# Mixture-of-experts output added onto the residual in DRAM by accumulating scatters, second-normalisation statistics one tile ahead, and a sample output projection in four column tiles

## What is computed

```python
x = LayerNorm(alpha*x + concat(A, B) @ w_o)                 # first normalisation
x = LayerNorm(alpha*x + HMoE(x))                            # second normalisation
# HMoE: top-1 of 4 expert groups, then top-2 of the 8 experts in that group
def expert_mlp(args):
    xb, e = args
    h = jax.nn.silu(xb @ w_gate[e]) * (xb @ w_up[e])
    return h @ w_down[e]
```

## Time and profile before

| | us |
|---|---|
| median of 3 runs (2557.14 to 2563.7) | 2558.19 |
| the profiled execution, its own time | 2568.49 |
| its span, first to last instruction | 2566.7 |
| TensorE busy in the span | 2293.2 (89%) |
| VectorE, ScalarE, GpSimd busy | 648.8, 334.0, 276.3 |
| bytes moved | 534.87 MB, mean 208 GB/s |

### The profile page before, as it was taken

One profiled execution on the slowest core, in us unless ns is written; L12 is line 12 of the kernel. 1 busy time (PEld: TensorE's weight loads), 2 busy tenths in 40 slices (PEclk: granted clock), 3 DMA queues, 4 the chain that ended last, 5 costly groups with the idle time before them and its releaser, 6 DMA issues.

```text
span 2566.7 us, 30101 instructions
## 1 busy us (share of the span) xinstructions
PE 2293.2 (89%) x10192; PEld 1523.8 (59%) x10192; DVE 648.8 (25%) x1249; ACT 334.0 (13%) x827; POOL 276.3 (11%) x440
## 2 busy tenths in 40 slices
PE   7999899997999999998289998999889999999962
PEld 5666556665666666665156664566566666666641
DVE  1211234453111111111811123343521111111127
ACT  2000122210011111110110001222101111111101
POOL 0100001111111111110211000111001111111101
PEclk8999888997999999999589998898889999999985
DMA  7201010025899999995541101101259999999952
GB/s 251 103 33 33 17 45 33 33 103 233 319 382 378 381 373 379 371 376 214 208 150 33 33 33 29 41 33 66 114 222 354 375 384 373 374 377 379 376 215 107
DMA packets 104080, 534.87 MB, mean 208 GB/s; under 512 B 16570, under 2 KB 25786, under 8 KB 87266
## 3 DMA queue, kind: packets, MB, share of 16 engines
q1 hardware_dynamic: 89154, 500.04, 50.7%
q0 software_dynamic: 14848, 33.84, 3.6%
HBM read 506.86 MB, written 49.82 MB: 217 GB/s over the span
## 4 chain that ended last, share of the span: by engine, by line
PE 86%; DVE 6%; issue 4%; DMA 2%; POOL 1%; ACT 1%; DVEq 0%; POOLq 0%; SPq 0%; ACTq 0%
PE ps L784 20%; PE ps L549 20%; PE ps L664 10%; PE ps L817 10%; PE ps L788 7%; PE ps L821 4%; PE ps L615 3%; PE ps L767 3%; PE ps L635 2%; PE ps L684 1%; PE ps L674 1%; DVE arena L1540 1%; DVE arena L1539 1%; DVE arena L1437 1%; PE ps L559 1%
## 5 line engine op out<-in xcount | busy, mean ns | idle before, releaser
L784 PE MATMUL ps<-arena 128*128 128x256 f32 x2304 | 512.2, 383 | 2.5 <-DVE arena L1437 2.5
L549 PE MATMUL ps<-arena 128*128 128x344 f32 x1728 | 508.2, 456 | 4.4 <-issue 3.5
L784 PEld LDWEIGHTS ps<-arena 128*128 128x128 f32 x2304 | 439.5, 192 | 88.3 <-issue 28.9
L549 PEld LDWEIGHTS ps<-arena 128*128 128x128 f32 x1728 | 329.9, 191 | 177.1 <-issue 9.1
L817 PE MATMUL ps<-arena 128*128 128x512 f32 x576 | 255.8, 597 | 20.3 <-ACT arena L1012 19.2
L664 PE MATMUL ps<-arena 128*128 128x512 f32 x512 | 241.8, 633 | 2.1 <-DVE arena L1248 2.1
L1448 DVE SCALAR_TENSOR_TENSOR arena<-ps,gates,arena 128x256 f32<-128x256 f32 (+1 forms) x128 | 61.4, 480 | 666.5 <-ACT arena L1007 666.5
L790 PE MATMUL ps<-arena 128*64 128x256 f32 x896 | 199.4, 381 | 0.0
L788 PE MATMUL ps<-arena 128*64 128x256 f32 x896 | 199.4, 381 | 0.0
L817 PEld LDWEIGHTS ps<-arena 128*128 128x128 f32 x576 | 106.5, 190 | 148.3 <-issue 122.1
L664 PEld LDWEIGHTS ps<-arena 128*128 128x128 f32 x512 | 102.8, 204 | 134.2 <-issue 134.2
(11 more groups left out here) (224 smaller groups left out, 1818.5 us busy)
## 6 DMA issues: line engine op xcount, KB each, us to landing
arena<-in_w_gate SPq DMA_DIRECT2D x64, 2048.0 KB, 7.7
arena<-in_w_up SPq DMA_DIRECT2D x64, 2048.0 KB, 15.4
arena<-in_w_down SPq DMA_DIRECT2D x64, 2048.0 KB, 13.3
arena<-in_w_in SPq DMA_DIRECT2D x36, 512.0 KB, 3.2
arena<-ytok SPq DMA_DIRECT2D x32, 512.0 KB, 9.8
arena<-in_w_o SPq DMA_DIRECT2D x2, 4096.0 KB, 18.4
arena<-out_y_all SPq DMA_DIRECT2D x16, 512.0 KB, 3.3
xs<-arena SPq DMA_DIRECT2D x16, 512.0 KB, 2.6
```

Of the source, the lines that this page charges most:

```text
L549: last = mm(ps[:, 3 * half + ch, 0:CH], wring[:, slot, k * P:(k + 1) * P], xT[:, k, ch * CH:(ch + 1) * CH], start=(k == 0), stop=(k == KD ...
L784: last = mm(ps[:, 2 + q, at_c:at_c + 256], xgT[:, slot, k], w[slot][:, k, cols], start=(k == 0), stop=(k == KD - 1))
```

## The change

- **Residual in DRAM.** `x1_out` writes each tile twice, to `xs1` and to the first half of `ytok`. The experts' scatters add onto those rows (`compute_op=ALU.add`), where they wrote to rows of their own before. A scatter waits until the one before it, from the other slot, has landed. Gates are multiplied by 1/alpha, and the second normalisation's epsilon is divided by alpha squared, so that the sum need not be scaled by alpha: normalising x1 + y/alpha gives the same as normalising alpha·x1 + y.
- **Second normalisation.** It loads one tile per token tile, where there were three, and has no additions. The statistics of tile p are computed ahead of the normalisation of tile p-1.
- **Sample output projection.** 32 matmuls of 256 columns, whose outputs lie at partitions 0, 32, 64 and 96 of one bank, so that they occupy four column tiles of the array; VectorE takes the four pieces in four instructions.
- **Index lists.** `as_rows` makes one list (2 instructions) where it made two (5 instructions).

```diff
@@ def x1_out
-                    sp.dma_start(a["xs1"][ds(b * P, rows), :], x1[0:rows, slot]).then_inc(s[f"x1_out{slot}"], 16)
+                    for dst in (a["xs1"], a["ytok"][0]):
+                        sp.dma_start(dst[ds(b * P, rows), :], x1[0:rows, slot]).then_inc(s[f"x1_out{slot}"], 16)
@@ sync, behind the last weights
-                for t in range(NB):
-                    sp.dma_start(x1r[t], a["xs1"][t * P:(t + 1) * P, :]).then_inc(s["l2_x"], 16)
@@ sync, second normalisation
-                    if t == NB:
-                        sp.dma_start(x1r[t], a["xs1"][r, :]).then_inc(s[f"l2_in{t}"], 16)
                     sp.dma_start(y0[t][0:rows], a["ytok"][0, r, :]).then_inc(s[f"l2_in{t}"], 16)
-                    sp.dma_start(y1[t][0:rows], a["ytok"][1, r, :]).then_inc(s[f"l2_in{t}"], 16)
@@ def out_project
+                    if rows < P:
+                        for k in range(KD):
+                            for n in range(4):
+                                last = mm(ps[32 * n:32 * n + rows, 6, 0:256], mix[:, k, 0:rows],
+                                          wo[:, k, n * 256:(n + 1) * 256], start=(k == 0), stop=(k == KD - 1))
+                        last.then_inc(s["wo_mm"], 1)
+                        return
@@ def residual
+                    if rows < P:
+                        for n in range(4):
+                            cols = slice(n * 256, (n + 1) * 256)
+                            ins = v.scalar_tensor_tensor(t1[r, cols], xres[r, slot, cols], ALPHA,
+                                                         ps[32 * n:32 * n + rows, 6, 0:256], ALU.mult, ALU.add)
...
@@ def as_rows
-                    first, rows_of = place_of[:, where], past_k[:, where]
-                    ts(first, values, float(NONE), None, ALU.add)
-                    ts(rows_of, first, float(T), float(-T), ALU.is_ge, ALU.mult)
-                    op(v.tensor_copy(sidx[:, where], first))
-                    tt(first, first, rows_of, ALU.add)
-                    op(v.tensor_copy(gidx[:, where], first))
+                    ts(place_of[:, where], values, float(NONE), None, ALU.add)
+                    op(v.tensor_copy(gidx[:, where], place_of[:, where]))
@@ second normalisation on VectorE
-                def layer_norm2(t, rows, p):
-                    r = slice(0, rows)
-                    dve.wait_ge(s[f"l2_in{t}"], BASE + (32 if t < NB else 48) * (l + 1))
-                    step.link(v.scalar_tensor_tensor(y0[t][r], x1r[t][r], ALPHA, y0[t][r], ALU.mult, ALU.add))
-                    step.link(v.tensor_tensor(y0[t][r], y0[t][r], y1[t][r], ALU.add))
+                def statistics2(t, r, p):
+                    dve.wait_ge(s[f"l2_in{t}"], BASE + 16 * (l + 1))
+                    dve.wait_ge(s["l2_stat"], BASE + NT * l + p)
                     for h in range(2):
                         step.mark(v.bn_stats(stat[r, 6 * h:6 * h + 6], y0[t][r, h * 512:(h + 1) * 512]))
...
+                statistics2(LN2_ORDER[0], rows_at[0], 0)
+                for p in range(1, NT):
+                    statistics2(LN2_ORDER[p], rows_at[p], p)
+                    normalised2(LN2_ORDER[p - 1], rows_at[p - 1], p - 1)
+                normalised2(LN2_ORDER[NT - 1], rows_at[NT - 1], NT - 1)
@@ def scatter
+                    if turn_other is not None:
+                        pool.wait_ge(s[f"sc_out{1 - slot}"], 16 * (NE // 2 * l + turn_other))
+                        settle(pool, s["pool_passed"])
-                    g.indirect_dma_start(out=a["ytok"].rearrange("k t d -> (k t) d"),
+                    g.indirect_dma_start(out=a["ytok"][0],
                                          out_offset=bass.IndirectOffsetOnAxis(ap=scol[0:rows, slot:slot + 1], axis=0),
-                                         in_=ys[0:rows, slot], in_offset=None,
-                                         bounds_check=2 * T - 1, oob_is_err=False).then_inc(s[f"sc_out{slot}"], 16)
+                                         in_=ys[0:rows, slot], in_offset=None, compute_op=ALU.add,
+                                         bounds_check=T - 1, oob_is_err=False).then_inc(s[f"sc_out{slot}"], 16)
```

More of the change, by code:

```diff
@@ L43 @@
 EPS = 1e-5
-STEPS_LAYER = 352
-OVER_STEPS = 26
+EPS2 = EPS / ALPHA ** 2
+STEPS_LAYER = 328
+OVER_STEPS = 23
 STEPS_POOL = 111
@@ L248, in build @@
         x1r = [at(32336 + 1024 * t, DM) for t in range(NB)] + [at(27496, DM, parts=NS)]
-        y_at = [8256 + 1024 * i for i in range(10)] + [21648 + 1024 * i for i in range(5)] + [28528 + 1024 * i for i in range(3)]
-        y0 = [at(y_at[2 * t], DM) for t in range(NT)]
-        y1 = [at(y_at[2 * t + 1], DM) for t in range(NT)]
+        y0 = [at(8256 + 1024 * t, DM) for t in range(NT)]
         x2 = at(16448, 2, DM)
@@ L279, in build @@
             "sync": (
-                "const_in", "copied", "ident_in", *(f"l2_in{t}" for t in range(NT)), "l2_x", "lnp_in", "ov_w", "small_out", "smp_in", "state_in", "w_in0",
+                "const_in", "copied", "ident_in", *(f"l2_in{t}" for t in range(NT)), "lnp_in", "ov_w", "small_out", "smp_in", "state_in", "w_in0",
                 "w_in1", "w_in2", "wd_in0", "wd_in1", "wg_in0", "wg_in1", "wo_in", "wu_in0", "wu_in1", "x1_out0",
@@ L1088, in _ @@
             for k in range(2):
-                step.mark(v.tensor_scalar(token[:, k, 1:NT], tokens1[:, 0:NB], float(k * T - 1 - NONE), None, ALU.add))
-                step.mark(v.tensor_scalar(token[:, k, 0:1], tokens1[:, NB:NT], float(k * T - 1 - NONE), None, ALU.add))
+                step.mark(v.tensor_scalar(token[:, k, 1:NT], tokens1[:, 0:NB], float(-1 - NONE), None, ALU.add))
+                step.mark(v.tensor_scalar(token[:, k, 0:1], tokens1[:, NB:NT], float(-1 - NONE), None, ALU.add))
             step.mark(v.tensor_scalar(bias_row[:], rank_desc[:], NE - FIRST + 0.5, 1e6, ALU.is_gt, ALU.mult))
@@ L1214, in residual @@
                     dve.wait_ge(s[f"xr_in{slot}"], BASE + 16 * ((5 - slot) * l + turn + 1))
-                    v.scalar_tensor_tensor(t1[r], xres[r, slot], ALPHA,
-                                           ps[r, 6:8, :].rearrange("p a b -> p (a b)"), ALU.mult, ALU.add
-                                           ).then_inc(s["ln_add"], 1)
+                    if rows < P:
[3 more added lines that the diff above has]
+                                                         ps[32 * n:32 * n + rows, 6, 0:256], ALU.mult, ALU.add)
+                            if n < 3:
+                                step.mark(ins)
+                        step.wait()
+                        settle(dve, s["dve_passed"])
+                        ins.then_inc(s["ln_add"], 1)
+                    else:
+                        v.scalar_tensor_tensor(t1[r], xres[r, slot], ALPHA,
+                                               ps[r, 6:8, :].rearrange("p a b -> p (a b)"), ALU.mult, ALU.add
+                                               ).then_inc(s["ln_add"], 1)
                     dve.wait_ge(s["ln_add"], BASE + m + 1)
@@ L1229, in scaled @@
                     dve.wait_ge(s["x1t_mm"], BASE + m - 1)
-                    dve.wait_ge(s[f"x1_out{slot}"], BASE + 16 * ((5 - slot) * l + turn))
+                    dve.wait_ge(s[f"x1_out{slot}"], BASE + 32 * ((5 - slot) * l + turn))
                     v.scalar_tensor_tensor(x1[r, slot], t1[r], rstd[r, 0, 0:1], lnp[r, 1], ALU.mult, ALU.add
@@ L1644, in gather, with scatter @@
                                          bounds_check=T - 1, oob_is_err=False).then_inc(s[f"xg_in{slot}"], 16)
-                def scatter(e, slot, turn, col, rows):
+                def scatter(e, slot, turn, col, rows, turn_other):
                     n = NE * l + e
@@ L1651, in scatter @@
                         settle(pool, s["pool_passed"])
-                    step.link(g.tensor_copy(scol[:, slot:slot + 1], sidx[:, ds(col, 1)]))
+                    step.link(g.tensor_copy(scol[:, slot:slot + 1], gidx[:, ds(col, 1)]))
                     pool.sem_inc(s["ys_free"], 1)
@@ L1712, in _ @@
                         settle(pool, s["pool_passed"])
[L1713 removed]
+                        g.indirect_dma_start(out=a["ytok"][0],
                                              out_offset=bass.IndirectOffsetOnAxis(ap=scol[:, 0:1], axis=0),
[L1715 to L1716 removed]
+                                             in_=ys[:, 0], in_offset=None, compute_op=ALU.add,
+                                             bounds_check=T - 1, oob_is_err=False).then_inc(s["ov_sc"], 16)
                         pool.wait_ge(s["ov_sc"], sent)
@@ L1728, in inverse2 @@
                     settle(pool, s["pool_passed"])
-                    step.link(g.tensor_scalar(rstd[r, p % 2, 1:2], mv[r, p % 2, 1:2], EPS, None, ALU.add))
+                    step.link(g.tensor_scalar(rstd[r, p % 2, 1:2], mv[r, p % 2, 1:2], EPS2, None, ALU.add))
                     g.tensor_tensor(rstd[r, p % 2, 0:1], rstd[r, p % 2, 1:2], mhalf[r], ALU.pow).then_inc(s["l2_rstd"], 1)
```

42 lines of the change are left out of this document (18 added, 24 removed).

## The result

| | before | after |
|---|---|---|
| median, us (lowest to highest of 4 runs each) | 2557.66 (2544.27 to 2563.7) | 2474.05 (2471.33 to 2476.03) |
| the profiled execution, its own time | 2568.49 | 2476.03 |
| its span | 2566.7 | 2474.2 |
| TensorE busy in the span | 2293.2 | 2266.5 |
| VectorE, ScalarE, GpSimd busy | 648.8, 334.0, 276.3 | 602.2, 334.1, 324.4 |

The ratio is 0.968, with a 95% interval of 0.9656 to 0.9703: 83.6 us less between the medians. The forecast was 2481 us, within 2468 to 2515.

The account below looks back on a forecast made before the run. TensorE was taken to bound the kernel, setting the expert pair's period with DMA engines 97% busy. The terms -60.4 - 17 - 1.2 + 2 = -76.6 us, say 77, off 2558.2 gave 2481 us, range 2468 to 2515.

Parts of the forecast that it names:

- Second normalisation: VectorE's second normalisation: a prompt tile falls from 7.61 to 4.24 us, saving 30.2 us a layer, 60.4 in two.
- Sample projection: First attention round: projection takes 5 us, not 14.87, so weighted values start sooner, saving 8.5 us a layer, 17 in two.
- Routing: `as_rows` ahead of the first gather: three chained instructions of 0.2 us go, saving 0.6 us a layer, 1.2 in all.
- Last scatter: End of each layer, 3.91 us on the chain: read-back costs perhaps 1 us more, 2 us in all.
- Scatters in the loop: Expert loop: 0.2 us of backlog a pair, 3 us over 14 pairs, within 6.4 us of slack, so no cost.
- Twice the plain scatter: Expert loop: an accumulating scatter costs double a plain one, adding 1.3 us a pair.
- the 1.1 us of idle time a pair: Expert loop: DMA engines 97% busy leave 3% of a pair's 36.23 us to absorb the added scatter work.
- The other sign: Expert loop: up weights should land after no more than 18 us.
- The mild DMA bound: Rival, expert loop: a pair needs 37.7 us, giving 2510 us, or 2526 with no room at all; chance 0.14.
- Stalling rows: Rival, expert loop: accumulating rows stall DMA engines, slower beyond 4.3 us more a pair, 2661 us at 1 us a row; chance 0.12.
- The column tiles overlap: Answers a rival: sample projection's tiles don't overlap or clock stays low, giving 2 of 17 us, 2496 us; chance 0.04.
- no load is late in the second normalisation: Answers a rival: next tile's load is late, each wait costing VectorE what it saved, possibly ending near the old time; chance 0.02.

Follow-up runs that it names:

- sample_undo: Changed kernel with the sample output projection back to two passes of 512 columns and one VectorE residual instruction: 2493.26 us, ratio to before 0.9769.
- plain_scatter: Changed kernel with plain, overwriting scatters in place of accumulating ones, all waits and loads kept: 2474.2 us, ratio to before 0.9685.
- ahead_only: Kernel before with only the second normalisation's statistics moved one tile ahead: 2540.78 us, ratio to before 0.9931.
- stats_inline: Changed kernel with each tile's statistics directly ahead of its own normalisation, not one tile ahead: 2487.77 us, ratio to before 0.9725.
- half_extra: Changed kernel with a second accumulating scatter, into another DRAM tensor, for slot 1's experts alone: 2500.27 us, one run.
- double_scatter: Changed kernel with every accumulating scatter issued a second time, into another DRAM tensor, with its own waits: 2569.29 us, ratio to before 1.0038.

## Why the prediction was right, and where its steps were off

- **Second normalisation, 60.4 us of gain forecast.** A tile takes 4.03 us, not 4.24: L1553 starts before L1549 has ended, for which the working had added 0.07 us where it should have taken 0.13 off. The stage is 36.6 us, not 38. With the last scatter in it, the working has 60.4 - 2 = 58.4 us and the two traces 61.8. VectorE started 1.2 us sooner behind the last scatter's landing, not 0.4. VectorE stayed the limit, as said; TensorE's eight transposes take 1.96 us of each tile.
- **Sample projection, 17 us.** 18.9 by the traces, 19.2 by undoing it (give or take 10). The four tiles do run at once. The projection took 5.52 us, not 5, since the clock stayed at 0.50 for about 3.9 us and not for the first 2. The softmax came next, as said, with a wait of 0.47 us.
- **Routing, 1.2 us.** Wrong. TensorE's first expert transposes now wait 6.45 us for the gather, where they waited 6.18. From the transposition ahead of the lists to these transposes it went from 11.34 to 11.01 us in layer 0 and from 11.60 to 11.66 in layer 1. In layer 0 the gather is issued 0.6 us sooner, as forecast, and takes 0.3 us longer to land (5.61 to 5.94 us; in layer 1 6.00 to 6.63). The step that failed is that TensorE's wait would end sooner by what the issue gained; the first weights are loading at that time, and the gather probably stands among them. That was not tried by itself.
- **Last scatter, 2 us.** The term was mis-sized: 2.3 and 2.1 us a layer longer, 4.4 in all. At 6.23 and 6.07 us the last scatter is over the 6 us that the text had named as a sign that the forecast is wrong.
- **Scatters in the loop, nothing.** The result held, by much less room than the text said, and in part by luck: the backlog is 0.4 us a pair on average, not 0.2, and 5.4 to 5.8 us at the end of the loop, not 3, of 6.4 that were free. "Twice the plain scatter" stands well enough: a plain one needs 1.6 us, not 1.3, and adding 1.2 to 1.9, not 1.3 (by q0's share 1.2 in the pair of 1009 us and 1.8 in the first full one, by the estimate above 1.2, by the period 1.9 at most). What was off is the other side, the 1.1 us of idle time a pair. It was read from the 97% of one pair late in the loop; the first full pair had 100% (the window above), and q0's share there was 9.6%, not 7.1%. The sign that the text asked for, q0's share up from 7.1% to about 11%, came (10.5%). The other sign, up weights landing after no more than 18 us, failed: 22.3 and 23.1 us at the end of the loops.
- **The rivals.** The mild DMA bound asked for 37.7 us a pair, and the need is 36.6. Stalling rows needed 4.3 us more a pair, and there are at most 1.9: with 8 rows for each engine at most 0.44 us a row (3.5 / 8) against 0.20 (1.6 / 8), where the break-even stood at 0.54. The column tiles overlap, and no load is late in the second normalisation.
- **What was in no term.** 61.8 + 18.9 + 0.3 = 81.0 us against 83.6 between the medians, so 2.6 us are left, within their spread. The two profiled executions differ by 92.5. Of that excess 8.6 us lie in layer 1's attention (280.44 to 271.84 us from first weighted values to first expert transposes), where the granted clock was 0.85 before and 0.88 after (`sample_undo` shows how far this goes from one execution to the next: 260.4 us at 0.91). Layer 0's attention was 1.6 us longer, at 0.87 in both. The profiled execution of before lay 10.3 us over its median, and the change does nothing to those matmuls, so I read the clock, not the change, as the cause; no run settles it. Another 4.3 us lie behind the last transposes: 9.3 us before, 5.0 after, with 8.6 in `plain_scatter`, 8.6 in `ahead_only` and 5.6 in `stats_inline`. What sets that stays open.

The Trainium skill, DMA: Bandwidth & Descriptors, Specifications, has about 358 GB/s of HBM for one core; by that rule every added byte would have cost time. The trace speaks against the rule as a limit here: slices of the span reach 387 GB/s, with no wait of TensorE. What ran short in the runs with added scatters is the engines' time: in `half_extra`, where TensorE waits for weights, they are 98% busy at 367 GB/s.

## What to carry to other kernels

Where TensorE and the DMA engines are both near the period of a loop, the busy share of one iteration doesn't tell how much room is left: `half_extra` waits for weights at 98%, and the kernel before did not wait at 95 to 100%. Read whether the landing times grow through the loop, against a kernel that has no such load and leaving out the loop's start, and set the whole growth against the slack. Read more than one iteration, too, where their loads differ. A period that is stretched by waits is no clean measure of the other engine's need if TensorE's clock falls after the waits; read the clock and the busy share beside it. Adding in DRAM took some 45 us of vector work off the chain for about 4 us on it, because it ran beside TensorE's work; the same transfer once more per pair gave it all back. And a result that another engine computes from a tile's statistics is best asked for one tile ahead: that alone was worth about 1 us on each of 18 tiles, in either kernel.

## What the runs showed of the hardware that was not expected

- The last accumulating scatter of a layer, 60 rows of 4 KB with next to nothing moving beside it, lands in 6.1 to 6.2 us, and a plain one in 3.9 to 4.0. In the loop an added accumulating scatter of 129 rows stretches a pair by 3.3 to 3.5 us and a plain one by 1.6. Part of the former is TensorE's clock after its waits; the queue's busy share puts the adding at 1.2 to 1.8 us of the 16 engines' time, and the estimate from `double_scatter` at 1.2.
- GpSimd takes 1.54 us on average to issue an accumulating scatter, and about 0.98 to issue a plain one. It cost nothing here, since GpSimd is 13% busy.
- The page's HBM counters do not show the read-back. Read fell from 506.86 to 489.95 MB, 16.9 MB, which is just the x1 and second-result loads that went; 2 x 2064 rows of 4 KB read back would be another 16.9. `plain_scatter`, which reads nothing back, has the same 489.95 MB. Written rose from 49.82 to 58.27 MB, the second write of x1.
- Four column tiles of 32 columns each ran at once with fp32 operands: 64 matmuls of 256 columns in 5.52 us, about 3.6 at full clock.
